# Delta rule: diagonal blocks of width 16 inverted on VectorE, three inverse levels on TensorE for four tiles together

## What is computed

```python
a = jnp.where(strict, jnp.einsum('bhncd,bhnsd->bhncs', kb, k) * decay, 0.0)
lower = a + jnp.eye(CHUNK, dtype=f32)
u = lax.linalg.triangular_solve(lower, v * beta[..., None], left_side=True, lower=True, unit_diagonal=True)
w = lax.linalg.triangular_solve(lower, kb * jnp.exp(gc)[..., None], left_side=True, lower=True, unit_diagonal=True)
...
v_new = u_i - jnp.einsum('bhcd,bhde->bhce', w_i, state)
o = (jnp.einsum('bhcd,bhde->bhce', q_dec_i, state) + jnp.einsum('bhcs,bhse->bhce', qk_i, v_new))
state = state * gl_i[..., None, None] + jnp.einsum('bhcd,bhce->bhde', k_dec_i, v_new)
```

## Time and profile before

| | us |
|---|---|
| median of 3 runs (2724.87 to 2727.11) | 2726.37 |
| profiled execution, its own time | 2724.91 |
| its span | 2723.3 |

### The profile page before, as it was taken

The page is one execution under the profiler, slowest core; times in us unless marked ns, Lnnn a source line. Parts: engine busy times, 40 slices in busy tenths (PEclk is TensorE's granted clock), DMA queues, the critical chain, the costliest instruction groups (busy, mean ns, idle before and its releaser), DMA issues.

```text
span 2723.3 us, 38374 instructions
## 1 busy us (share of the span) xinstructions
PE 2625.3 (96%) x13534; PEld 2181.5 (80%) x13534; DVE 1445.8 (53%) x2206; ACT 993.5 (36%) x1797; POOL 129.9 (5%) x157
## 2 busy tenths in 40 slices
PE   5999999999999899999999989999999998999998
PEld 4887778888888778888888877888888787788887
DVE  6666464364655646435465654634556555563454
ACT  4455332232445433222344543322234554322222
POOL 0011000000001100000000210000000011000000
PEclk9999999999999999999999999999999999999999
DMA  4210122224321012323332002232333200223242
GB/s 184 93 47 1 47 87 99 95 98 149 138 87 38 1 63 85 100 93 118 129 136 89 24 1 70 93 100 93 135 117 130 83 17 1 85 93 100 93 139 77
DMA packets 62027, 233.48 MB, mean 86 GB/s; under 512 B 7232, under 2 KB 7232, under 8 KB 61248
## 3 DMA queue, kind: packets, MB, share of 16 engines
q1 hardware_dynamic: 55728, 202.83, 22.2%
q0 software_dynamic: 6160, 28.84, 2.8%
HBM read 223.26 MB, written 8.39 MB: 85 GB/s over the span
## 4 chain that ended last, share of the span: by engine, by line
PE 75%; issue 20%; DVE 2%; ACT 2%; POOL 1%; POOLq 0%; DVEq 0%
PE ps L1143 72%; PE ps L1270 1%; PE ps L1365 1%; ACT xi L610 1%; PE ps L1345 1%; POOL xi L333 0%; PE ps L1329 0%; ACT dt L631 0%; DVE h_l L1057 0%; DVE sm L841 0%; DVE h_l L1082 0%; DVE at L864 0%; ACT h_h L638 0%; DVE xi L839 0%; ACT dt L474 0%
## 5 line engine op out<-in xcount | busy, mean ns | idle before, releaser
L1143 PE MATMUL ps<-h_h,w_h 128*128 128x512 f32 x2016 | 797.2, 395 | 22.7 <-DVE h_l L1082 8.6
L1143 PE MATMUL ps<-h_l,w_h 128*128 128x512 f32 x2016 | 786.7, 390 | 0.0
L1143 PE MATMUL ps<-h_h,w_l 128*128 128x512 f32 x2016 | 786.5, 390 | 0.0
L708 DVE TENSOR_TENSOR w_l<-stage,w_h 128x1024 fp32r<-128x1024 f32 (+1 forms) x385 | 467.9, 1215 | 312.6 <-ACT w_h L371 300.0
L371 ACT CAST w_h<-stage 128x1024 fp32r<-128x1024 f32 (+1 forms) x385 | 399.9, 1039 | 551.9 <-PE ps L1143 543.2
L1143 PEld LDWEIGHTS ps<-h_h,w_h 128*128 128x128 f32 x2016 | 379.3, 188 | 116.3 <-DVE h_l L1082 11.5
L1143 PEld LDWEIGHTS ps<-h_l,w_h 128*128 128x128 f32 x2016 | 379.8, 188 | 80.7 <-issue 3.8
L1143 PEld LDWEIGHTS ps<-h_h,w_l 128*128 128x128 f32 x2016 | 379.6, 188 | 80.0
L1143 PE MATMUL ps<-ff_h,w_h 128*128 128x512 f32 x1024 | 400.0, 391 | 0.0
L1143 PE MATMUL ps<-ff_h,w_l 128*128 128x512 f32 x1024 | 398.4, 389 | 0.0
L1143 PE MATMUL ps<-ff_l,w_h 128*128 128x512 f32 x1024 | 398.4, 389 | 0.0
(11 more groups left out here) (161 smaller groups left out, 2314.1 us busy)
## 6 DMA issues: line engine op xcount, KB each, us to landing
stage<-w SPq DMA_DIRECT2D x385, 512.0 KB, 3.3
x_next<-x POOLq DMA_DIRECT2D x20, 512.0 KB, 6.4
xs<-x POOLq DMA_DIRECT2D x4, 2048.0 KB, 8.8
out<-xs POOLq DMA_DIRECT2D x32, 256.0 KB, 2.3
bia<-bias POOLq DMA_DIRECT2D x1, 1536.0 KB, 6.5
cst<-con SPq DMA_DIRECT2D x1, 896.0 KB, 4.7
prm<-par SPq DMA_DIRECT2D x1, 38.5 KB, 1.9
```

Source lines behind the costliest of these rows:

```text
L708: dve.tensor_tensor(w_l[:, b, 0:k], stage[:, s, 0:k], w_h[:, b, 0:k].bitcast(F32), ALU.subtract).then_inc(w_lo.sem, 1)
L1143: return pe.matmul(o, a, b, start=start, stop=stop)
```

## The change

The inverse is no longer begun at width 2. The blocks of width 16 on the diagonal (128 of them a group: 4 tiles, 4 heads, 8 blocks) are brought by 32x32 transposes on VectorE into a layout with one block in each partition (`gather`), where 17 instructions invert them all (`block_inverse`), and transposes bring them back (`scatter`) into `ti` and `xi`, which GpSimd has set to zero. TensorE then has three levels (`masked`, `update`, `turn`), for all four tiles together; the last one works on 64 columns and has no transposes. All four gate units stand behind the queries. Decay, gram and query-key product of all four tiles are between the query units (`tile_products`). The transposes of keys and values of tiles 0 and 1 stand between the gate units, of tiles 2 and 3 behind them. The tiles `eg`, `dt`, `gb` and others lie in the memory of `xs`, so the load of `xs` is issued by GpSimd late in the stage. The output projection begins with the attention's half of its first two units.

```diff
-LEVELS = 6
+BLOCK = 16
+QUADS = 4
+LEVELS = 3
...
-U_BA, U_AV, U_AK, U_AQ, U_Z = 14, 15, 16, 17, 21
+U_BA, U_AV, U_AK, U_AQ, U_Z = 12, 13, 14, 15, 19
...
+        def lev(t):
+            return 4 + t
...
+                for t in range(TILES):
+                    q_tile = qkvz[:, 0:4, t * P:t * P + P]
+                    wt(B["egl"], t)
+                    wt(B["q2_r"], t)
+                    wt(B["p_kq"], t)
+                    nc.gpsimd.tensor_tensor(q_tile, q_tile, eg[:, t % 2], ALU.mult).then_inc(B["qd_r"].sem, 1)
+                pool.wait_ge(normed.sem, normed.after(g, NORMS + 1))
+                pool.nop(nofuse=True)
+                nc.gpsimd.memset(ti[:], 0.0).then_inc(zeroed.sem, 1)
+                nc.gpsimd.memset(xi[:], 0.0).then_inc(zeroed.sem, 1)
+                for n in range(14):
+                    probabilities(n)
+                pool.wait_ge(B["mlo"].sem, B["mlo"].after(g, 2))
...
+                    decay(t)
+                    key_log(t)
+                    query_square(t)
+                    delta(t)
...
+                act.preload_act_table_set("silu_and_others")
+                for m in range(GATE):
+                    if m < GATE - 1:
+                        split_hi(g, CONV, U_Z + 1 + m + 1 - CONV) if m < 2 else split_hi(g, CONV, U_PAD - CONV, 1)
+                    gate(m)
+                act.preload_act_table_set("natural_log_exp_and_others")
...
+                    dve.scalar_tensor_tensor(out=at_[:, t], in0=heads(GRAM), scalar=-1.0, in1=dt_[:, a],
+                                             op0=ALU.mult, op1=ALU.mult).then_inc(B["at_r"].sem, 1)
+                    wt(B["p_kq"], t)
+                    dve.tensor_tensor(qk[:, t], heads(KQ), dt_[:, a], ALU.mult).then_inc(B["qk_r"].sem, 1)
...
+                def gather():
+                    own(B["at_r"], g, TILES)
+                    for n in range(QUADS):
+                        r = slice(32 * n, 32 * n + 32)
+                        dve.transpose(by_block(tmp[r]), quad(at_, r)).then_inc(blk_in.sem, 1)
+                    own(blk_in, g, QUADS)
+                    to = gb[:, 0:BLOCK * BLOCK].rearrange("p (j i) -> p j i", i=BLOCK)
+                    both = by_block(tmp[:]).rearrange("p i b j -> p b j i")
+                    block_step(dve.tensor_scalar(to, both[:, 0], prm[:, C_BLK:C_BLK + 1], None, ALU.mult))
+                    block_step(dve.scalar_tensor_tensor(out=to, in0=both[:, 1], scalar=prm[:, C_BLK + 1:C_BLK + 2], in1=to,
+                                                        op0=ALU.mult, op1=ALU.add))
+                def scatter():
+                    flip = d1[:, 0].rearrange("p h c -> p (h c)")
+                    rows = tb[:, 0:BLOCK * BLOCK].rearrange("p (r c) -> p r c", c=BLOCK)
+                    for b in range(2):
+                        own_half = prm[:, C_BLK + b:C_BLK + b + 1]
+                        dve.tensor_scalar(by_block(tmp[:])[:, :, b], rows.rearrange("p r c -> p c r"), own_half, None,
+                                          ALU.mult).then_inc(blk_ext.sem, 1)
+                        dve.tensor_scalar(by_block(flip)[:, :, b], rows, own_half, None, ALU.mult).then_inc(blk_ext.sem, 1)
+                    own(blk_ext, g, 4)
+                    dve.wait_ge(zeroed.sem, zeroed.after(g, 2))
+                    for n in range(QUADS):
+                        r = slice(32 * n, 32 * n + 32)
+                        dve.transpose(quad(ti, r), by_block(tmp[r])).then_inc(blk_out.sem, 1)
+                        dve.transpose(quad(xi, r), by_block(flip[r])).then_inc(blk_out.sem, 1)
...
+                def block_inverse():
+                    block_step(dve.tensor_copy(blocks(tb, 1)[:, :, 1, 0], blocks(gb, 1)[:, :, 0, 1]))
...
+                    block_step(outer(y, a[:, :, 0, 2:4], x2[:, :, 0, 0:2]))
+                    block_step(outer(z, a[:, :, 1, 2:4], x2[:, :, 1, 0:2]))
+                    block_step(dve.tensor_tensor(y, y, z, ALU.add))
+                    block_step(outer(z, x2[:, :, 2:4, 2], y[:, :, 0]))
+                    block_step(outer(z2, x2[:, :, 2:4, 3], y[:, :, 1]))
+                    block_step(dve.tensor_tensor(x2[:, :, 2:4, 0:2], z, z2, ALU.add))
...
+                    for b in (4, 8):
+                        n = 8 // b
+                        a, x2 = blocks(gb, b), blocks(tb, b)
+                        prod = tmp[:, 0:n * b * b * b].rearrange("p (m i c j) -> p m i c j", m=n, i=b, c=b)
+                        y = yb[:, 0:n * b * b].rearrange("p (m i c) -> p m i c", m=n, i=b)
+                        cube = [P, b, b, b]
+                        def dot(m, left, right):
+                            return dve.tensor_tensor(prod[:, m], left.unsqueeze(2).to_broadcast(cube),
+                                                     right.unsqueeze(1).to_broadcast(cube), ALU.mult)
+                        for m in range(n):
+                            block_step(dot(m, a[:, m, 0:b, b:2 * b].rearrange("p j i -> p i j"),
+                                           x2[:, m, 0:b, 0:b].rearrange("p j c -> p c j")))
+                        block_step(dve.tensor_reduce(y, prod, AX.X, ALU.add))
+                        for m in range(n):
+                            block_step(dot(m, x2[:, m, b:2 * b, b:2 * b], y[:, m].rearrange("p k c -> p c k")))
+                        block_step(dve.tensor_reduce(x2[:, :, b:2 * b, 0:b], prod, AX.X, ALU.add))
+                    assert nb[0] == blk.per_group, nb
...
+                gather()
+                block_inverse()
+                split_lo(g, CONV, U_Z + 3 - CONV)
+                scatter()
...
+                    if l < LEVELS - 1:
+                        m = dve.tensor_tensor(dl[:, t].rearrange("p (h c) -> p h c", h=HEADS),
+                                              ps[:, lev(t), 0:256].rearrange("p (h c) -> p h c", h=HEADS),
+                                              cst_lev(cst, l).unsqueeze(1).to_broadcast([P, HEADS, 64]), ALU.mult)
+                    else:
+                        m = dve.tensor_copy(dl[64:P, t], ps[64:P, lev(t), 0:256])
+                    m.then_inc(y_ready.sem, 1)
...
+                token_rows(0)
+                split_lo(g, CONV, U_PAD - CONV, 1)
+                token_rows(1)
+                token_rows(2)
+                mask(0, 0)
+                mask(0, 1)
+                token_rows(3)
+                mask(0, 2)
+                mask(0, 3)
+                attend(0)
+                for t in range(TILES):
+                    extend(0, t)
+                attend(1)
...
+                    four(heads(ROW), lambda o, h: mm(o, cst[0:64, K_SEL + h, :], tile), B["p_gr"])
+                    if t:
+                        wt(B["at_r"], t - 1)
+                    four(heads(GRAM), lambda o, h: mm(o, k[:, h], k[:, h]), B["p_gg"])
+                    if t:
+                        wt(B["qk_r"], t - 1)
+                    four(heads(KQ), lambda o, h: mm(o, k[:, h], q[:, h]), B["p_kq"])
...
+                for m in range(GATE):
+                    if m < 2:
+                        pe.wait_ge(copied.sem, copied.after(g, 5 + m))
+                    else:
+                        pe.wait_ge(z_ready.sem, z_ready.after(g, m - 1))
+                    unit(g, CONV, U_Z + m - CONV, A0 + (U_Z + m) % 2, hid)
+                    if 0 < m < GATE - 1:
+                        token_rows(m - 1)
...
+                def masked(l, t):
+                    if l:
+                        pe.wait_ge(x_ready.sem, x_ready.after(g, (l - 1) * TILES + t + 1))
+                    elif t == 0:
+                        pe.wait_ge(blk_out.sem, blk_out.after(g, blk_out.per_group))
+                        wt(B["at_r"], TILES - 1)
+                    elif t == 1:
+                        wt(B["eg_r"], TILES - 1)
+                    elif t == 2:
+                        pe.wait_ge(z_ready.sem, z_ready.after(g, GATE))
+                    o = ps[:, lev(t), 0:256]
+                    if l < LEVELS - 1:
+                        four(o.rearrange("p (h n b) -> p h n b", h=HEADS, b=BLOCK << l),
+                             lambda o, h: mm(o, at_[:, t, h], first_half(ti[:, t, h], l)), p_y)
+                    else:
+                        pe.nop(nofuse=True)
+                        four(o[64:P].rearrange("p (h c) -> p h c", h=HEADS),
+                             lambda o, h: mm(o, at_[0:64, t, h, 64:P], ti[0:64, t, h, 0:64]), p_y)
+                def update(l, t):
+                    pe.wait_ge(y_ready.sem, y_ready.after(g, l * TILES + t + 1))
+                    o = ps[:, lev(t), 256:512].rearrange("p (h c) -> p h c", h=HEADS)
+                    if l < LEVELS - 1:
+                        four(o, lambda o, h: mm(o, xi[:, t, h], dl[:, t, 64 * h:64 * h + 64]), p_u)
+                    else:
+                        pe.nop(nofuse=True)
+                        four(o[0:64], lambda o, h: mm(o, dl[64:P, t, 64 * h:64 * h + 64], xi[64:P, t, h, 64:P]), p_u)
+                def turn(l, t):
```

(52 more changed lines are left out.)

839 lines of the change are left out of this document (365 added, 474 removed), and 4 rows, old and new, of the table STEPS.

## The result

The changed kernel takes 2622.26 us (median of 4 runs, 2619.74 to 2624.41), the kernel before 2725.68 in the same session: a ratio of 0.962, 95% interval 0.9603 to 0.9636. The forecast was 2616 us in a range of 2575 to 2655. The profiled execution takes 2619.7 us with a span of 2618.2, so 105.1 us of span are gone, 26.3 a group.

The account below looks back on a forecast made before the run. TensorE, busy for 2625.3 of 2723.3 us, was taken as the bound. Removed 47.7 less added 20.0 us gave net 27.7 a group, 111 in all: a median of 2616 us, range 2575 to 2655.

Parts of the forecast that it names:

- (1): Levels on TensorE: two full levels and a narrower third replace twelve levels of a pair, removing 30.3 us a group.
- (3, 4): Rebuilt stage on TensorE: eight kinds of wait go, 13.4 us a group, and the slow clock behind the longest, 2.2.
- (a): Ahead of the fourth gate block TensorE waits for VectorE's gather, inverse, scatter and rows: 9.4 us a group added.
- (b): Behind the wait ahead of the fourth gate block the TensorE clock falls: 2.2 us a group added.
- (c): Levels and attention: attention steps with less cover make TensorE wait, 5.0 us a group added, between 0 and 12.
- (d): The first norm sum stands behind the cumulated decays on VectorE: 1.1 us a group added.
- (e): End of the stage: last attention part uncovered, 1.5 us, and last delta tile outlasting its cover, 0.8; 2.3 added.
- Costs at nothing: GpSimd's zeroing, the late load of `xs` and 8 unchanged ScalarE table loads were to add no time.
- the lock: Rival at the gather: GpSimd's zeroings lock VectorE out, starting the chain 8 us later; 2646 us, chance 0.06.
- set the pace: Rival behind the gate blocks: the attention sets the pace, 15 us more a group; 2675 us, chance 0.08.
- The dear chain: Rival: VectorE's gather, inverse and scatter cost twice their price, 16 us longer a group; 2680 us, chance 0.08.

Follow-up runs that it names:

- e5: The changed kernel with 16 matmuls of 512 columns, results unread, filling TensorE's wait ahead of the fourth gate block; 2612.21 us.
- e9: The changed kernel with only the first output projection unit beginning with the attention's half, the second whole behind it; 2636.55 us.
- e6: The changed kernel with GpSimd's two zeroings started later, so they lie fully over the gathering transposes; 2620.28 us.
- e4: The changed kernel with the second of the three levels left out on every engine, the inverse then incomplete; 2592.4 us.
- e8: e7 with the inverse's transpose made by TensorE and copied by ScalarE, fourth-unit low weights inside the inverse, tile 0 value and key rows before the scatter; 2575.97 us.
- e3: The changed kernel with 60 matmuls of 512 columns, results unread, in TensorE's wait ahead of the fourth gate block (mis-sized); 2759.65 us.
- e2: The changed kernel with the fourth gate block ahead of tile 1's transposes on TensorE, its low weights made right behind the gather; 2608.63 us.
- e7: e2 with VectorE gathering the blocks ahead of the third gate unit's low weights; 2596.84 us.
- e1: The changed kernel with the four transposes that gather the diagonal blocks made twice, same result; 2638.64 us.

## Why the prediction was right, step by step

Group 1, where the sum is read, saved 28.2 us from its first mean to the next; the four average 26.3, and the forecast was 27.7. The mechanism was right: time left with the levels and the waits, and one wait for VectorE's chain came instead. One term was mis-sized.

- **Levels (1).** Removed: forecast 30.3, measured 32.2. The two full levels take 18.2 us as they should. The third, whose shape no row showed, takes 4.0 us (64 records in 2.01 and 2.00), below both bounds of 4.7 and 7.3: 64 weight columns with 64 rows go at 0.063 us a record. Size off by 2 us, mechanism right.
- **Waits and clock of before (3, 4).** 13.4 and 2.2 us went, as forecast; no run puts these waits back, so that the new order removed them is read from the two lists alone. The 13.4 hold a wait of 1.5 us that ends at 978.84, behind the start of the output projection, and so lies outside the stage.
- **The wait (a): the term that was mis-sized.** Arrival of TensorE: 22.2 us behind the end of the fourth query block, exact. VectorE is through with the third unit's low part at 12.7 (13.4 forecast). Then the gather takes 5.7 us (3.4), the inverse 7.0 (6.0), the low part 1.2 (1.2), the scatter 9.1 (5.9). The step that failed is the price of the transposes: 0.6 us from start to start, by a multiplication of the same count. They take 1.13 us in the gather and 0.96 in the scatter, and the twelve are 5.1 us dearer than forecast. Most of the 1.0 us in the inverse are its two multiplications of 512 elements, 1.04 and 1.07 us where 0.73 was allowed. With the 0.8 us of the key rows, which e5 shows, the term is 15.1 us instead of 9.4, inside the bounds of 7 to 17. The sentence that the sum would stay within a microsecond by the Trainium skill's rate (Vector Engine (DVE) Microarchitecture Reference, 3.8 The reshape front-end and per-opcode configuration) misled: the measurement decides, and these transposes of 512 elements last half as long again as a multiplication of 512 (0.99 to 1.10 us against 0.69). Each of them also reads or writes one side with a step between elements (`quad`), and no run separates the instruction from the step.
- **The clock behind it (b).** 2.0 us against 2.2, and e5 shows the cause. The Trainium skill (TensorE: Matmul & The Clock Gate, Why this matters for your kernels) warned of idle gaps; e5 (2.0 us back with the gap filled) and e9 (1.3 us lost behind a new one) agree with it.
- **Levels and attention (c).** 5.0 us were allowed. TensorE is not busy for 4.3 us of the last two stretches, of which 1.5 belong to the end, so 2.8. Steps 4 and 5 back to back cost nothing that the list shows; the two dear ones are steps 16 and 17.
- **First norm sum (d)** 1.1, measured 1.0. **The end (e)** 2.3, measured 1.5 + 0.2.
- **Costs at nothing.** The zeroing took 1.8 us each instead of up to 5.1, and e6 shows that even its overlap is free. The load of `xs` appears in no wait of TensorE. ScalarE's table loads are 17 before and after, four a group and not 8; that they do not change is right.

Sum with the measured terms: removed 32.2 + 1.8 + 13.4 + 2.2 = 49.6; added 15.1 + 2.0 + 2.8 + 1.0 + 1.7 = 22.6; net 27.0. It reaches past the stage on both sides of the comparison (1.5 and 0.2 us), so it belongs beside the 28.2 of group 1, and 1.2 us stay unexplained. The forecast's nearness is in part luck. The wait was 5.7 us dearer than forecast, while (1) and (c) together were 4.1 us better and (b), (d) and (e) 0.9. Of the rivals, e6 excludes the lock for the transposes. Copies with one operand meet it, by the Trainium skill (SBUF — State Buffer, Who interferes with whom), only in the fast two-port modes, which the prediction leaves out; no run here puts a copy of this chain beside the zeroing. The attention does not set the pace (42.05 of 43.25 us), but e4 shows it is near. The dear chain came true at 1.4 times its price (21.9 us for gather, inverse and scatter against 15.3), not at twice.

## What to carry to other kernels

Work moved from a full engine to a half-idle one is paid at the place where its result is first needed: count both engines' way to that place, and put there whatever does not need the result. Here the change itself left 46 us on the table (e8): by the order of a gate block, of the gather, of low weights and of value and key rows, and by four transposes on VectorE in place of which TensorE could transpose. An instruction that no row shows should be priced with a bound above its neighbours of equal size, and one mis-priced instruction counts as often as it stands in the chain: here twelve times.

Each wait of about 3 us and more that was followed here cost more than its length, because the clock fell: 2.0 us on top of 14.3 (e5), 1.3 on top of 2.9 (e9), 1.7 on top of 3.2 (e8). Filling such a wait with work, even with work that nobody reads, shows what the clock costs.

## What was not expected of the hardware

- A 32x32-blocked transpose on VectorE of 32 partitions by 512 elements takes 0.99 to 1.10 us, a two-operand multiplication of 512 elements on 128 partitions 0.69. It costs that for a quarter of the partitions. One side of each of these transposes is read or written with a step between elements.
- Multiplications of 512 elements that read with broadcasts and steps inside a block cost 1.05 to 1.14 us (`tmp<-gb,tb` and `tmp<-tb,yb`), those of 64 elements 0.27. Which of the two makes them dear was not tried.
- A 32-bit matmul with the identity and 512 columns takes 0.86 us (e3), against 0.23 for one matmul of a weight unit with 512 columns.
- The runs of kernels with a wait of 7.5 to 9 us spread over 10 to 12 us (e2, e7), those that kept TensorE busy or had only a short wait over 2.4 to 4.6 (e5, e8). The length of the wait is not the reason: the longest, 18.7 us, has the smallest spread, 1.9 us (e1). What decides how long the clock stays down was not tried.
